# Output product of layer one as seven products of quarters, and the modulation's sums moved to earlier stages

## What is computed

```python
for l in range(2):
    mod = silu(c) @ w_ada[l] + b_ada[l]                 # (1, 6144)
    shift, scale, gate = jnp.split(mod, 3, axis=-1)
    h = rms_norm(x, norm_g[l]) * (1.0 + scale[:, None, :]) + shift[:, None, :]
    proj = h @ w_in[l]                                  # 2048 -> 6144
    u, z_s, q, k, v, z_a = jnp.split(proj, splits, axis=-1)
    y_s = s5_mixer(u, ..., w_glu[l], b_glu[l]) * silu(z_s)   # state space, 64 groups
    y_a = diff_attention(rope(q), rope(k), v, ...) * silu(z_a)
    y = jnp.concatenate([y_s, y_a], axis=-1) @ w_out[l] # 2048 x 2048, the product changed
    x = x + gate[:, None, :] * y
```

## Time and profile before

| | |
|---|---|
| Time, median of 3 runs | 4313.69 us (4313.32 to 4317.63) |
| Profiled execution, its own time | 4312.6 us |
| Its span | 4310.8 us |
| TensorE busy | 4123.4 us, 96% of the span |
| VectorE busy | 2438.4 us, 57% |
| ScalarE, GpSimd busy | 807.5 us, 495.4 us |
| Chain that ended last | PE 82%, DVE 13%, ACT 2% |

### The profile page before, as it was taken

The page is one execution under the profiler, slowest core; times in us unless marked ns, Lnnn a source line. Parts: engine busy times, 40 slices in busy tenths (PEclk is TensorE's granted clock), DMA queues, the critical chain, the costliest instruction groups (busy, mean ns, idle before and its releaser), DMA issues.

```text
span 4310.8 us, 41307 instructions
## 1 busy us (share of the span) xinstructions
PE 4123.4 (96%) x16042; PEld 2761.2 (64%) x16042; DVE 2438.4 (57%) x4211; ACT 807.5 (19%) x1450; POOL 495.4 (11%) x816
## 2 busy tenths in 40 slices
PE   6899999999999999999999999999999999999999
PEld 3565544444447555444458668878788877788888
DVE  5576536664533564356766566465655467766643
ACT  1222201132011321011321122121211122220000
POOL 0133211111211331111111000000000101100000
PEclk8899999999999999999999999999999999999999
DMA  9533332334552333333345332222121233334433
GB/s 323 186 117 100 115 122 93 129 110 147 147 184 67 115 105 117 113 118 113 124 128 171 113 100 72 64 67 66 59 74 59 89 107 115 123 100 136 138 103 103
DMA packets 370192, 499.29 MB, mean 116 GB/s; under 512 B 44379, under 2 KB 279118, under 8 KB 369486
## 3 DMA queue, kind: packets, MB, share of 16 engines
q1 hardware_dynamic: 289984, 340.16, 24.4%
q0 software_dynamic: 38608, 125.86, 9.2%
q10 hardware_dynamic: 41406, 30.63, 2.3%
HBM read 462.51 MB, written 34.08 MB: 115 GB/s over the span
## 4 chain that ended last, share of the span: by engine, by line
PE 82%; DVE 13%; ACT 2%; issue 1%; DMA 1%; ACTq 0%; POOL 0%; DVEq 0%; SPq 0%
PE bank L108 80%; DVE tring L132 2%; DVE tring L117 2%; DVE tring L123 2%; PE bank L111 2%; ACT tring L114 1%; DVE wring L117 1%; DMA yaT<-in_w_ada 1%; DVE tring L120 1%; DVE dring L120 1%; DVE bank L117 1%; ACT L114 1%; DVE dring L117 0%; DMA SS<-in_w_ada 0%; DVE sring L138 0%
## 5 line engine op out<-in xcount | busy, mean ns | idle before, releaser
L108 PE MATMUL bank<-region_b,wring 128*128 128x256 f32 (+2 forms) x4448 | 1323.7, 451 | 7.8 <-ACT region_b L114 6.6
L108 PE MATMUL bank<-region_a,wring 128*128 128x256 f32 (+1 forms) x3232 | 1084.9, 489 | 29.0 <-DVE wring L117 29.0
L108 PEld LDWEIGHTS bank<-region_b,wring 128*128 128x128 f32 (+1 forms) x4448 | 829.6, 190 | 411.6 <-issue 331.2
L108 PEld LDWEIGHTS bank<-region_a,wring 128*128 128x128 f32 x3232 | 614.8, 194 | 416.7 <-issue 338.2
L147 POOL DMA_DIRECT2D side<-in_w_ada x384 | 208.7, 544 | 1466.7 <-DVE tring L123 937.4
L123 DVE SCALAR_TENSOR_TENSOR tring<-side,cact,tring 128x512 f32<-128x512 f32 x360 | 305.2, 848 | 76.4 <-DMA side<-in_w_ada 40.0
L114 ACT ACT_TABLE_LOAD x160 | 205.3, 1283 | 360.7 <-DVE sring L120 283.7
L117 DVE TENSOR_TENSOR tring<-bank,tring 128x256 f32<-128x256 f32 (+1 forms) x229 | 100.9, 441 | 298.8 <-PE bank L108 295.5
L108 PE MATMUL bank<-wring,region_b 128*128 128x512 f32 (+1 forms) x640 | 265.1, 570 | 0.5 <-ACT region_b L114 0.5
L117 DVE TENSOR_TENSOR wring<-wring 128x1024 f32<-128x1024 f32 (+1 forms) x213 | 234.7, 1102 | 17.4 <-PE bank L108 8.5
L114 ACT ACTIVATE tring<-bank 128x512 f32<-128x512 f32 (+1 forms) x166 | 81.4, 493 | 822.5 <-PE bank L108 502.1
(11 more groups left out here) (285 smaller groups left out, 4303.3 us busy)
## 6 DMA issues: line engine op xcount, KB each, us to landing
wring<-in_w_in SPq DMA_DIRECT2D x180, 1024.0 KB, 5.3
side<-in_w_ada POOLq DMA_DIRECT2D x384, 256.0 KB, 3.2
wring<-in_w_out SPq DMA_DIRECT2D x48, 1024.0 KB, 8.5
yaT<-in_w_ada SPq DMA_DIRECT2D x16, 1024.0 KB, 8.7
wring<-in_w_glu SPq DMA_DIRECT2D x16, 1024.0 KB, 7.2
tring<-x_saved SPq DMA_DIRECT2D x48, 256.0 KB, 3.0
gring<-in_w_ada POOLq DMA_DIRECT2D x43, 256.0 KB, 2.9
SS<-in_w_ada SPq DMA_DIRECT2D x8, 1024.0 KB, 8.2
```

Source lines behind the costliest of these rows:

```text
L108: return self.e.matmul(*a, **k) if self.e else self
```

## The change

Layer zero's output product goes through `fast`, as layer one's does. The activation sums are made in another order, for which `Split` has the new field `over`: the first three go to region_a and to scratch of layer one's state space (SS), and the fourth is written over the right half of the activations themselves, when nothing needs them any more (`quarter_last`). Em of layer one holds the third weight sum. The factor of `interleave` with `state_space_params(1)` goes from 0.2 to 0.23, since a job now has 7 steps and not 8. `carried[0]` in layer zero goes from 1.25 to 1.7 beside the state space, from 1.7 to 2.3 beside attention, and from 1.8 to 0.4 beside the output product. The list `y_parts` and the tiles `gluT` and `s3_glu` are made and not used by any product; the new condition on `p` in `fast` meets only jobs of 8 tiles of input features, of which none has anything to advance.

```diff
@@ -233,6 +233,7 @@
     sums: Any
     free: Callable
     chunk: dict
+    over: bool = False
 
     def quarter(self, i, k):
         r, c = divmod(i, 2)
@@ -325,12 +326,20 @@
             m["k"] = [sb(f"k{l}{b}", [P, 2, T], att) for b in range(2)]
             m["v"] = [regions[l][:, 0:4, :], sb(f"v{l}", [P, TT, 512], att)]
             m["wT"] = [sb(f"wT{l}{b}", [P, TT, T], att) for b in range(2)]
+            gluT = sb(f"gluT{l}", [P, 2, 4, 256], att)
+            m["gluT"] = [regions[l][:, HT:HT + 4, 256:512], gluT[:, 0, :, :], gluT[:, 1, :, :],
+                         regions[l][:, 6:8, :].rearrange("p k (h t) -> p (k h) t", h=2)]
+            m["s3_glu"] = Room([sb(f"s3_glu{l}", [P, 4, P], att)])
             att.close()
             if l:
                 wide = ExitStack()
                 outT = sb("outT", [P, 4, HT, 256], wide)
                 m["outT"], m["s3"] = [outT[:, i, :, :] for i in range(4)], Room([sb("s3_out", [P, HT, P], wide)])
                 wide.close()
+                lay[0]["outT"] = [regions[0][:, 0:HT, 256:512],
+                                  *(regions[0][:, HT + 4 * i:HT + 4 * i + 4, :].rearrange("p k (h t) -> p (k h) t", h=2) for i in range(2)),
+                                  SS[:, :, :, :, :].rearrange("p i q c n -> p (i q c n)").rearrange("p (k t) -> p k t", k=HT)]
+                lay[0]["s3"] = Room([m["Em"].rearrange("p q c n -> p (q c n)").rearrange("p (k n) -> p k n", k=HT)])
             layer_mem.close()
             lay.append(m)
         first.close()
@@ -502,7 +511,7 @@
                 if p == 4:
                     for step in late:
                         do(*step)
-                if p != 3:
+                if p != 3 and (job.kt > HT or p in (2, 6, 7)):
                     follow(None)
                     carry()
                     yield
@@ -1025,9 +1034,12 @@
                 for j in range(2):
                     temps.give("old", l, n0 // P + j)
 
+        y_parts = [Split(f"y{l}", HT, lambda r, k, n, l=l: xTs[l][:, HT + 4 * r + k:HT + 4 * r + k + n, :],
+                         lambda k, l=l: [ssm_d.of("yT", l, k)], lay[l]["gluT"], lambda l=l: passed("ssm", l), {}, True) for l in range(2)]
+
         def block_one(l):
             beside = beside_states(l)
-            carried[0] = 1.25
+            carried[0] = [1.7, 1.25][l]
             if l:
                 norm_one()
                 group = open_group([u_job(l, 0)])
@@ -1052,25 +1064,28 @@
             turn_u(l, 0)
             interleave(state_space(l), beside, [73, 77][l] / 79)
             do("fence", "ssm", l)
-            carried[0] = 1.7
+            carried[0] = [2.3, 1.7][l]
             run_all(pair_products(l, 0))
             run_all(value_products(l, 0))
             interleave(attention(l), beside_attention(l), 45 / 37, 32, 1.6)
             do("fence", "att", l)
             finish_behind(3 - 2 * l)
-            carried[0] = 1.8
+            carried[0] = [0.4, 1.8][l]
             yaT, xT = lay[l]["yaT"], xTs[l]
             def ready(k):
                 return [taken_d.of("ys", l, k)] if k < HT else [att_d.of("ya", l, k - HT)]
+            parts = Split(f"out{l}", KT, lambda r, k, n: (yaT if r else xT)[:, k:k + n, :], ready, lay[l]["outT"],
+                          lambda: passed("att", l), {}, l == 0)
+            late = [("quarter_rest", parts, k, 4) for k in (0, 4)]
             if l == 0:
-                interleave(add_gated(l, d["w_out"][l], lambda k: xT[:, k, :] if k < HT else yaT[:, k - HT, :], ready),
-                           state_space_params(1), 0.2)
+                late += [("quarter_last", parts, k, 4) for k in (0, 4)]
+            for k in range(0, HT, 4):
+                quarter(parts, k, 4)
+            out_products = add_gated(l, d["w_out"][l], None, ready, parts, lay[l]["s3"], late)
+            if l == 0:
+                interleave(out_products, state_space_params(1), 0.23)
             else:
-                parts = Split("out", KT, lambda r, k, n: (yaT if r else xT)[:, k:k + n, :], ready, lay[l]["outT"],
-                              lambda: passed("att", l), {})
-                for k in range(0, HT, 4):
-                    quarter(parts, k, 4)
-                run_all(add_gated(l, d["w_out"][l], None, ready, parts, lay[l]["s3"], [("quarter_rest", parts, k, 4) for k in (0, 4)]))
+                run_all(out_products)
             finish_behind(2 - 2 * l)
 
         OFF, o_ = {}, 0
@@ -1317,7 +1332,7 @@
         do("gates")
         h_parts = Split("h", KT, lambda r, k, n: regions[1][:, HT * r + k:HT * r + k + n, :], lambda k: [h_ready.of(2, k)],
                         [regions[1][:, 0:HT, 256:512], *(pairs_of(regions[0][:, 4 * i:4 * i + 4, :]) for i in range(3))],
-                        lambda: [x_stored.of(2)], {})
+                        lambda: [x_stored.of(2)], {}, True)
         for k in range(0, HT, 4):
             quarter(h_parts, k, 4)
             do("quarter_rest", h_parts, k, 4)
@@ -1992,7 +2007,7 @@
                 for k in range(k0, k0 + n):
                     room(s.ready(k))
                     room(s.ready(s.kt // 2 + k))
-                if s.name == "h":
+                if s.over:
                     dve.tensor_tensor(t2, b12, b11, SU).then_inc(*d_step.up())
                     own()
                     dve.tensor_tensor(t2, b22, t2, SU).then_inc(*quarters_summed.up(s.name, 1, k0))
@@ -2009,7 +2024,8 @@
 
             def quarter_last(s, k0, n):
                 b11, b12, _, _ = quarters_of(s, k0, n)
-                room(passed("raw"))
+                if s.name == "h":
+                    room(passed("raw"))
                 dve.wait_ge(*quarters_summed.of(s.name, 2, k0))
                 dve.tensor_tensor(s.sums[0][:, k0:k0 + n, :], b12, b11, SU).then_inc(*quarters_summed.up(s.name, 0, k0))
```

## The result

The changed kernel takes 4355.7 us (median of four runs, 4354.9 to 4356.7), the kernel before 4315.3 in the same set. The ratio is 1.0093, with a 95% interval of 1.0081 to 1.0105. I had forecast 4312, with a range of 4301 to 4320. The change costs 40 us, where I expected a gain of 2. (The product changed is that of the first layer, "layer zero" in the text; only the title counts the layers from one.)

The account below looks back on a forecast made before the run. TensorE, busy for 96% of the span, was taken to bound the kernel. The terms summed to -1.8 us against the profiled 4312.6, giving 4312 for the median of runs; own range 4306 to 4319, 8-in-10 range 4301 to 4320.

Parts of the forecast that it names:

- The matmuls: Layer zero's output product: 896 records of 256 tokens replace 512 of 512, taking 26.4 us away.
- The start: Start of layer zero's output product: TensorE waits for VectorE's activation and weight sums, losing 4.7 us.
- Part 0: Third block of the product: VectorE's first parameter run delays fold 0; 8.3 us wait plus 2.3 for the clock, +10.6.
- Part 1: Fourth block of the product: the second parameter run delays weight sum 2; 6.9 us wait, with the clock +9.2.
- The -6.3: Layer zero's output product: the old wait of 3.7 us for the parameters goes, with its slow clock.
- Part 2 and the next run: Fourth to fifth block: the third parameter run delays a weight sum, +1.9 us; the next run costs nothing or some tenths.
- Weights: Layer zero's output product: weights, two 1 MB slots a block in 24 us instead of 27, given little chance of bounding it.
- rival C: Nothing is gained because another wait, such as the weights, bounds the output product: 4317 us, chance 0.06.
- Sums beside the attention: Attention: modulation sums moved ahead of the product delay some turns behind the weighing, +3.5 us.
- rival B: Slower through the attention: moved sums stay ahead of most turns, with slow clock behind longer waits; +15, 4328 us, chance 0.12.
- The end: End of the output product: the last output tile waits for fold 3 before its residual, +0.5 us.
- Beside the state space: State-space stretch: about 11 more modulation sums on a VectorE idle for 121 us, put at 0.5 us.

Follow-up runs that it names:

- e1: Changed kernel with each block's weight loads issued on SyncE's queue ahead of the fetches of saved x in layer zero's output product; 4330.5 us, ratio 1.0031.
- e9: Changed kernel with the last third of layer one's state-space parameters, which takes six temporary tiles, issued behind the whole product; 4332.9 us, ratio 1.0035.
- e2: Changed kernel with the three modulation rates put back to 1.25, 1.7 and 1.8 steps; 4344.5 us, ratio 1.0062.
- e3: Kernel before the change with only the modulation rates set to the new 1.7, 2.3 and 0.4 steps; 4333.8 us, ratio 1.0032.
- e8: e3 without the loads of layer one's shift and scale tiles or VectorE's waits for them, the sums still made; 4317.6 us, ratio 1.0001.
- e7: e4 with modulation rates of 1.7 steps in the state space, 1.7 in the attention and 1.4 in the product; 4310.5 us, ratio 0.9986.
- e5: e4 with the modulation's old rates of 1.25, 1.7 and 1.8 steps; 4300.5 us, ratio 0.9959.
- e12: e11 with modulation rates of 1.3 steps in the attention and 2.6 in the product; 4316.6 us, ratio 1.0001.
- e11: e6 with VectorE's two copies completing the parameter row issued one step earlier, every later piece moving one place on; 4309.2 us, ratio 0.9985.
- e10: e5 with layer one's state-space parameters in three long runs, not six pieces; 4310.5 us, ratio 0.9987.
- e6: e5 with parameter pieces only at two of a block's seven steps and the turns of C in two pairs; 4292.5 us, ratio 0.9943.
- e4: e1 with layer one's state-space parameters in six pieces, not three, and the interleave factor at 0.28; 4316.3 us, ratio 0.9996.

## Why the prediction was wrong, by its steps

- **The matmuls, -26.4**: right. The trace of before has 512 records of 512 tokens for the stage's 256 matmuls, that of after 896 of 256 tokens for 448. Sixteen of after step by 3.45 us (1088.82 to 1092.27), 0.216 each. The mean duration of one record is more than its step, 0.60 us for 0.429 before, and some 0.38 for 0.216 in the products with yaT after, so the time is counted by steps.
- **The start, +4.7**: right to a tenth. The Em product comes at 1088.82, which is 22.0 us behind 1066.84; five products are 17.3.
- **Part 0, +10.6**: measured 7.97 + 1.9 of clock = 9.9. **Part 1, +9.2**: 6.42 + 2.7 = 9.1. Both right. The -6.3 ahead of them is the old wait of 3.72 and the 2.6 by which the 16 records behind it are longer, 9.61 for 7.03; after, TensorE has no wait at the turn of that row.
- **Part 2 and the next run, +1.9**: 3.48 + 1.8 = 5.3. I had said "too short for the clock"; it was not.
- **Weights, 0**: wrong, and the largest error: 18.2 + 7.2 = 25.4. I gave rival C 0.06 with the sentence "Layer one has the same need and no wait for it". The need is the same, what stands ahead of it in SyncE's queue is not: in layer one no parameters hold six temporary tiles. The failed step is that I counted the weights' transfer and not SyncE's order; of the queues I looked at GpSimd's alone. e1 and e9 show the cause from both sides.
- **Sums beside the attention, +3.5**: wrong by 10 and more. It is 13.5 in the attention (after against e2), and 1.8 ahead of it: in both together waits grew by 7.2 and the clock took 6.5 more. e3 gives 16 us in the time of the kernel for the rates alone. The number of sums and most of the turns were right. The failed sentence is "GpSimd's queue is stepped past as well ... behind such a step stand its state-space sums, which TensorE needs a step later only". In the attention its rotations stand ahead of the loads; VectorE waits for the tile, with all that TensorE needs behind it. I priced a sum by its 0.85 us, and e8 shows the loads and their landings to be the larger part (11 of 16.4 us). The number of sums alone is no measure: e7's attention is 6.1 us longer than e5's at the same number, and e12's is 1.4 longer than e11's with 16 fewer. The case itself (slower through the attention, +15) was rival B, at 0.12; both that and C came true, together.
- **The end, +0.5**: 1.2, since the first product of layer one waits 7.23 for 5.99. With the old rates (e2, e5, e10) it waits 5.99 again, so this is not fold 3, which I named.
- **Beside the state space, +0.5**: it is 1.4. Two marks in TensorE's time, one ahead of that stretch and one at its end, before and then after:

```profile
161.30 1.84 PE L108 MATMUL bank<-ones,tring 128*128 128x1 f32 x16
...
499.52 0.60 PE L111 MATMUL bank<-const,region_a 128*128 128x128 f32 x4
```

```profile
162.68 1.84 PE L108 MATMUL bank<-ones,tring 128*128 128x1 f32 x16
...
502.29 0.60 PE L111 MATMUL bank<-const,region_a 128*128 128x128 f32 x4
```

They stand 338.2 us apart before and 339.6 after. All kernels with 1.25 steps there have 338.1 to 338.3, all with 1.7 have 339.6 to 339.9, and TensorE's one wait there, for ScalarE, is 3.7 us in the first and 4.6 in the second. From there to the wait near 675 us it is 174.0 before and 175.8 after. So of the 18.9 us that the product starts later, 1.4 are the spread of the program's start (161.30 and 162.68), 1.4 the state space, 1.8 the stretch ahead of the attention, and 14.3 the attention itself.
- **Without the two failed steps** the sum was -1.8 - 3.5 - 0.5 = -5.8. e10, which has neither the queue's stop nor the new rates, measures -5.5. That is closer than the terms deserve: it also has the modulation in the product, and the 3 us or so gained in layer one. The match of the sum is in part luck.
- **The signs named beforehand**: two of the three for "wrong" came, waits of over 3 us in other blocks and an attention longer by over 10 us.

On the clock, I had to choose between a price for each wait and one in proportion. In the product the waits of 3.48, 6.03, 6.05, 6.10, 6.42 and 7.97 us lost 1.8, 2.7, 2.9, 1.6, 2.7 and 1.9, which is 2.3 on average, the price I took. It does not grow with the wait. For shorter waits it is not fixed: behind 2.26 us at 1063.20 in e5, 32 records take 9.12 where 7.07 is usual; behind 2.45 us at 1147.47 in e6 they take 7.17, and the granted clock stays 1.00. Behind the one of 6.42:

```profile
1170.00:1175.00 5.00, 3.84 (x9) 3.13 (x10) 2.33 (x2) 0.00 (x0) 0.00 (x0) 0.50 0.02 1
1175.00:1180.00 5.00, 5.00 (x21) 4.25 (x21) 0.76 (x2) 0.00 (x0) 0.00 (x0) 0.86 0.02 3
```

The granted clock is 0.50 over the first 5 us and 0.86 over the next. That a longer wait costs no more clock was my estimate, and the six losses above agree with it. Nor do the runs show a length of wait from which the loss begins. "Some 2 us" (rival B) and "too short for the clock" (part 2) were my estimates from waits of 2.39 and 3.72 us. Behind 1.88 us at 1124.28 in e11, 16 records take 5.36 where 3.62 is usual, with a clock of 0.66 from 1124 to 1129; behind 3.13 us at 1202.67 in e5, 32 take 7.17, with 1.00 from 1202 to 1207.

## What to carry to other kernels

Before you call a transfer hidden, read the issuing engine in time, with the length of each stop, and ask for every stop what stands behind it and what it will wait for once the work beside it is shorter. Here a stop of 12 to 15 us cost nothing in blocks of 27 us; in blocks of 24, with the tiles as scarce, it grew to 23 to 32 and cost 8 us each time. The same holds for GpSimd's stop in the attention, 17.5 us before and 18.5 after. And price a moved operation by all that it can be made to wait for in its new place (a tile's landing, issued by a third engine's queue), not by its duration; here, work put beside TensorE's did best in short pieces, at places chosen against its next need, and a shift by one place (e11) lost more than the pieces had won.

## What the runs showed of the hardware

In e4, behind 1208 us, two weight sums of VectorE (2.06 and 1.95 us) and two wide operations of GpSimd (1.28 and 1.90 us) run beside each other, and each takes longer than where the other engine has no such operation. VectorE in time:

```profile
1209.11 2.06 DVE L117 TENSOR_TENSOR Em<-wring 128x1024 f32<-128x1024 f32 x1
1211.20 1.95 DVE L117 TENSOR_TENSOR wring<-wring 128x1024 f32<-128x1024 f32 x1
```

and GpSimd in time:

```profile
1208.81 1.28 POOL L117 TENSOR_TENSOR tring<-r,const_one 128x512 f32<-128x512 f32 x1 [0.17 <-POOL W L117]
1210.16 1.90 POOL L117 TENSOR_TENSOR tring<-th,const_one 128x512 f32<-128x512 f32 x1
```

Alone, the weight sums take 1.22 us and GpSimd's two operations 1.04 each (e11, from 1235.46 and 1236.57, while VectorE waits). One after the other that makes 4.52; here the four took 4.34 from first start to last end, hardly less. No run isolates a cause. The wait of 3.38 us just behind holds 1.6 us of it.
